# Down weights of the experts asked for by ScalarE on its own DMA queue, gate and up weights by SyncE

## What is computed

```python
def hier_moe(h, w_rg, b_rg, w_re, b_re, w_gate, w_up, w_down):
    ...                                    # router: 1 group of 4, then 2 experts of its 8
    hid = jax.nn.silu(jnp.einsum('td,edf->tef', t, w_gate)) * jnp.einsum('td,edf->tef', t, w_up)
    out = jnp.einsum('tef,te,efd->td', hid, combine, w_down)
...
x = x + hier_moe(rmsnorm(x, g_ffn), w_rg, b_rg, w_re, b_re, w_gate, w_up, w_down)
x = x + jax.nn.sigmoid(rmsnorm(x, g_ple) @ w_ple_gate) * (p @ w_ple_proj)
return rmsnorm(x, g_final)
```

## Time and profile before

| | |
|---|---|
| median of 3 runs | 1341.33 us (1340.49 to 1343.56) |
| the profiled execution | 1340.05 us, its span 1338.3 us |
| mean granted TensorE clock | 0.947 of full |
| TensorE matmul busy | 1222.7 us, 91% |
| ScalarE busy | 236.8 us, 18% |
| moved by DMA | 191.81 MB, mean 143 GB/s |
| expert stage | from about 955 us to about 1244 us of the span |

### The profile page before, as it was taken

The page is one execution under the profiler, slowest core; times in us unless marked ns, Lnnn a source line. Parts: engine busy times, 40 slices in busy tenths (PEclk is TensorE's granted clock), DMA queues, the critical chain, the costliest instruction groups (busy, mean ns, idle before and its releaser), DMA issues. The chain is left out here.

```text
span 1338.3 us, 14817 instructions
## 1 busy us (share of the span) xinstructions
PE 1222.7 (91%) x5963; PEld 856.8 (64%) x5963; DVE 482.4 (36%) x1053; ACT 236.8 (18%) x414; POOL 102.4 (8%) x163
## 2 busy tenths in 40 slices
PE   5999999999999999999999999997599878888596
PEld 4668888877775888877777787444355434444242
DVE  3235375144204356324221111255233222222475
ACT  3232121010013221003022000011022111122122
POOL 0000000000000000000000000001223222221000
PEclk9999999988999999989899999988599998999798
DMA  6111110234031100231354414304299999995300
GB/s 235 63 63 63 63 64 0 81 96 128 21 125 63 64 31 33 79 98 35 112 169 157 157 63 157 141 28 164 76 364 387 387 389 392 402 388 191 134 32 35
DMA packets 78492, 191.81 MB, mean 143 GB/s; under 512 B 10918, under 2 KB 29174, under 8 KB 70232
## 3 DMA queue, kind: packets, MB, share of 16 engines
q1 hardware_dynamic: 72724, 181.76, 37.3%
q0 software_dynamic: 5440, 8.94, 2.1%
q10 hardware_dynamic: 260, 0.16, 0.0%
HBM read 180.71 MB, written 17.98 MB: 148 GB/s over the span
## 5 line engine op out<-in xcount | busy, mean ns | idle before, releaser
L962 PE MATMUL ps<-arena,weights 128*128 128x272 f32 x2560 | 611.2, 400 | 5.1 <-ACT arena L641 2.5
L962 PEld LDWEIGHTS ps<-arena,weights 128*128 128x128 f32 x2560 | 493.3, 194 | 119.1 <-issue 12.2
L1408 PE MATMUL ps<-arena 128*64 128x256 f32 x1024 | 131.8, 416 | 33.0 <-DMA arena<-in_w_up 32.9
L1408 PEld LDWEIGHTS ps<-arena 128*64 128x64 f32 x1024 | 77.3, 149 | 76.6 <-DMA arena<-in_w_up 35.8
L672 DVE TENSOR_SCALAR arena<-arena 128x544 f32<-128x544 f32 x32 | 14.2, 444 | 203.6 <-ACT arena L570 111.9
L1128 PE MATMUL ps<-weights,arena 128*128 128x512 f32 (+1 forms) x160 | 69.5, 638 | 2.5 <-PEq L428 2.5
L1500 DVE TENSOR_SCALAR arena<-arena 64x256 f32<-64x256 f32 x32 | 9.3, 291 | 159.8 <-ACT arena L1461 152.4
L1669 PE MATMUL ps<-weights,arena 128*128 128x512 f32 (+1 forms) x160 | 64.8, 606 | 1.3 <-DVE arena L1732 1.3
L1421 PE MATMUL ps<-arena 128*64 128x512 f32 x256 | 61.9, 604 | 0.6 <-DVE arena L1524 0.6
L975 PE MATMUL ps<-weights,arena 128*128 128x512 f32 x128 | 55.3, 592 | 0.0
L997 PE MATMUL ps<-arena 128*128 128x64 f32 x448 | 54.2, 275 | 0.6 <-DVE arena L784 0.6
(11 more groups left out here) (221 smaller groups left out, 1034.2 us busy)
## 6 DMA issues: line engine op xcount, KB each, us to landing
weights<-in_w_in SPq DMA_DIRECT2D x18, 2048.0 KB, 8.2
arena<-in_w_gate SPq DMA_DIRECT2D x32, 1024.0 KB
arena<-in_w_up SPq DMA_DIRECT2D x32, 1024.0 KB
arena<-in_w_down SPq DMA_DIRECT2D x32, 1024.0 KB
arena<-in_x_prompt SPq DMA_DIRECT2D x8, 512.0 KB, 8.9
arena<-in_state_hgrn SPq DMA_DIRECT2D x8, 512.0 KB, 9.9
out_hgrn_sample<-arena SPq DMA_DIRECT2D x8, 512.0 KB, 3.6
weights<-in_w_br_b SPq DMA_DIRECT2D x2, 2048.0 KB, 7.9
```

Of the source, the lines that this page charges most:

```text
L962: ins = mm(ps[:, b + s, 0:HF], W[:, c % 2, k, col:col + P], src[:, k, s * HF:s * HF + HF], start=(k == 0), stop=(k == KT - 1))
L1408: ins = mm(ps[u * UP:u * UP + CAP, 2 + s, 0:DE], xgT[s][:, k, :], w[e % 4][:, k, :], start=(k == 0), stop=(k == KT - 1))
```

## The change

ScalarE now issues the down weights, at the end of its turn e, right behind its half of `rows_out(e)`, and only for e + 4 < 32. SyncE's list loses every down load and every wait on `dn_ready`. The waits that guard the buffers are the same in meaning: `rows_out(e)` has waited for `down(e)`.

```diff
@@ sync
                 for e in range(NE - 4):
                     sp.wait_ge(gu_ready, e + 1)
                     load_gate_up(sp, e + 4)
-                    if e:
-                        sp.wait_ge(dn_ready, e)
-                        load_down(sp, e + 3)
-                sp.wait_ge(dn_ready, NE - 4)
-                load_down(sp, NE - 1)
                 sp.wait_ge(gu_ready, NE - 3)
                 sp.dma_start(wpp, a["w_ple_proj"][0].rearrange("(k p) n -> p k n", p=P)).then_inc(pp_loaded, 16)
@@ scalar
                     if e + 2 < NE:
                         copy_t(e + 2)
                     rows_out(e)
+                    if e + 4 < NE:
+                        load_down(act, e + 4)
```

## The result

The changed kernel takes 1351.58 us (median of 5 runs, 1348.51 to 1352.81) against 1341.33 us (5 runs, 1339.31 to 1349.12), a ratio of 1.0075 with a 95% interval of 1.0042 to 1.0108. That is 10.2 us slower where 2.7 us were forecast, and above the range of 1338.5 to 1349.0. Timed again among the experiments it came out at 1.0066 (1.0032 to 1.0100). The sign was right, the size was not.

The account below looks back on a forecast made before the run. The prediction took the expert stage to be bound by DMA bytes. Issue changes counted 0 and the order of the last bytes +2.7 us, so 1341.3 + 2.7 = 1344.0 us, range 1338.5 to 1349.0.

Parts of the forecast that it names:

- What bounds the kernel: Expert stage, the only place touched: bound by DMA bytes, engines busy all the time at 389 GB/s from 1030 to 1220 us.
- The requests, ScalarE's issues: Expert stage: removing SyncE's 28 issues and waits is worth 0; ScalarE's 28 issues of 0.4 us lie beside other work, 0.
- Served one for one, both queues move on by one expert in the same time, and neither runs away: Two weight queues in the expert stage: equal packet counts, so only one more MB gets ahead of the last gate and up pair.
- The term of +2.67 us: End of the expert stage: one more MB ahead of expert 31's gate and up moves their landing from 1218.30 to 1220.97.
- Rival 1: Expert stage: down weights run three experts ahead, all landing before the last pair, and TensorE's 6.83 us binds; +6.8 us, chance 0.22.
- Rival 4, a lower rate: Expert stage: two weight streams with different piece sizes lose one more per cent of rate, 2.5 us, in all +5.2; chance 0.10.
- waits still on gate and up alone: Sign expected in the profile after: TensorE's waits remain on gate and up only, with gate_up(31) starting 2 to 3 us later.

Follow-up runs that it names:

- two equal queues: Against the kernel before: SyncE issues gate and half of down, ScalarE up and the other half, in the old order; ratio 1.0078, with earlier gathers 1.0019.

## Why the prediction was wrong

- *What bounds the kernel*: right. The DMA engines are full in both traces, and almost all of the difference lies in the stage. (TensorE falls to 7 or 8 tenths in five of the seven slices with a 9 for DMA, not in all of them; nothing hangs on it.)
- *The requests, ScalarE's issues*: right. Nothing was won on SyncE; ScalarE's issues of 0.37 us lie under other work and are not held.
- *"Served one for one, both queues move on by one expert in the same time, and neither runs away"*: the step that failed. One for one is right, shown by the equal counts of three kernels with 272, 288 and 320 packets of down per expert and by the alternation of the packets themselves. The count of packets was wrong: the completion packets take turns too. They give 288 to 272, a gain of 6% per expert, and the last pair of gate and up lands with two more transfers before or beside it, not one. The term of +2.67 us measured 5.6 (7.5 less the later end of 1.9). With those two transfers moved back the last pair landed 5.1 us sooner after gate_up(29)'s pair (11.5 against 16.6, both with earlier gathers), about the 5.3 of two transfers. TensorE could not use all of it, since the pairs before were late as well. The sum took the delay as one at the end of the stage; in fact gate_up(29) was 7 us late already (243.0 against 235.9).
- *Rival 1* named this end of the order, for another reason (turns equal in bytes). Its price was 6.8 us, because it let all down weights be three experts ahead and TensorE bind; in fact down caught up slowly and TensorE still waited 2.42 us for the last pair. With pieces of 8 KB the rival's picture came true, at 6.5 us.
- *Rival 4, a lower rate*: 2.5 us guessed, 1.4 to 1.9 measured as the later landing of w_ple_proj; the forecast had put this at nothing. The packets took 0.7 to 1.0% longer (8 KB: 333 and 334 ns on average in two traces before, 337 and 336 after). Why is open: it went away with earlier gathers in one kernel and stayed in another. What is shown is that the gathers belonged in my sum and were not there. Three queues instead of two take turns, and TensorE waited for gathers 14 or 15 times instead of 4 to 7, while the prediction had "waits still on gate and up alone". I had taken GpSimd's queue for untouched. In the changed kernel earlier gathers were worth 0.7 to 0.8 us (one trace); with two equal queues 11.7 by the traces and about 8 by the ratios.
- The two together are 7.0 to 7.5 us in the stage. The median moved by 10.2 us, by 9.1 in the second timing (1347.67 against 1338.57; 8.8 by the ratio), with intervals of 5.6 to 14.5 and 4.3 to 13.4 us. The 2 or 3 us between trace and medians are inside them and not explained further.

The Trainium skill (DMA: Bandwidth & Descriptors, Queues, rings and completion order) says that an engine drains a packet of typically 9 to 17 descriptors before it turns to the next queue. If a transfer's share were one turn, gate's 8 + 1 packets per engine would stand against down's 16 + 1, and the counts would be 9 to 17. They are 1 to 1 here, and the turns that can be followed on one engine are a single packet of the records long in 96% of the cases; the measurement decides against that size of turn for these queues. The rule of the same page of the Trainium skill that several issuing engines save only the sequencer's time (Issuing engines are not separate DMA queues) holds for the rate, 387 against 389 GB/s, but not for the time: which bytes come first changed, and that cost 5.6 us.

## What to carry to other kernels

In a stage bound by DMA the second queue gave no bandwidth here; it replaced the order of the bytes by one in turns, packet for packet, completion packets included. Count what each queue has per step, and look at what stands behind the last load that compute needs. When you move it back, look at the loads before it too: the engine that waited may bind next, as TensorE did here with 6.77 us per expert. And list everyone who shares the DMA engines, small gathers above all: with one more full queue they landed later here (9.0 us instead of 7.1), and an issue that had been early enough no longer was.

## What the runs showed of the hardware that I had not expected

Small completion packets take a full turn: 16 of them per transfer shifted the shares of two queues from 0.500 to about 0.52 of the bytes, though each lasts only some 9 ns in the records. A DMA share of 1.02 is no proof of a healthy rate; it stood beside 391, 387, 379 and 293 GB/s. The lowest came with transfers over 64 partitions instead of 128 with the same pieces of 4 KB. The 16 DMA engines don't finish together: their 16 completions of w_ple_proj lie 14.5 us apart in the kernel before (246.3 to 260.8 us) and 18 us in the changed one, and the slowest, 8.4 and 9.0 us behind the median, sets the landing. The granted clock of the stage does not follow the late gathers: from 1000 to 1200 us it was 0.90 in the two equal queues with 18 such waits and 0.93 with 2, but 0.94 in the changed kernel with 15 and 0.92 in the same kernel with 1.
